# Offsets of the norms and the pool bias added to x by DMAs instead of by GpSimd

## The reference

```python
def reference(x, ...):
    for i in range(DEPTH):
        j = i // N_MIXERS
        if i % N_MIXERS == 0:
            mix = ssd_mixer(x, ...)
        else:
            mix = pool_mixer(x, pool_w[j], pool_b[j], pool_scale[j])
        x = layer_norm(DEEPNORM_ALPHA * x + mix, ln_mix_g[i], ln_mix_b[i])
        x = layer_norm(DEEPNORM_ALPHA * x + sq_relu_mlp(x, mlp_w1[i], mlp_w2[i]), ln_ffn_g[i], ln_ffn_b[i])
    return x
```

## Time and profile before

| | us |
|---|---|
| median of 3 runs | 2206.31 |
| lowest and highest | 2205.95, 2207.38 |
| profiled execution, its own time | 2205.52 |
| profiled execution, span | 2203.8 |

### The profile page before, as it was taken

The page is one execution under the profiler, slowest core; times in us unless marked ns, Lnnn a source line. Parts: engine busy times, 40 slices in busy tenths (PEclk is TensorE's granted clock), DMA queues, the critical chain, the costliest instruction groups (busy, mean ns, idle before and its releaser), DMA issues.

```text
span 2203.8 us, 31261 instructions
## 1 busy us (share of the span) xinstructions
PE 2163.3 (98%) x10626; PEld 1817.0 (82%) x10626; DVE 1439.6 (65%) x1778; ACT 1109.6 (50%) x1549; POOL 234.0 (11%) x172
## 2 busy tenths in 40 slices
PE   9999999999999999999999999989999999999997
PEld 7788888888887778888888888867888888888886
DVE  6787867858768855555565655696565655555656
ACT  5677747757665544444353443446343443443433
POOL 0213322303310500000000000033000000000001
PEclk9999999999999999999999999999999999999999
DMA  8969896988956665555555555446555555555553
GB/s 272 252 202 237 237 278 180 238 230 227 239 183 221 203 212 184 182 200 176 205 190 190 195 185 180 168 152 227 191 191 190 200 181 187 194 180 200 190 191 115
DMA packets 246963, 443.96 MB, mean 201 GB/s; under 512 B 14048, under 2 KB 49040, under 8 KB 245216
## 3 DMA queue, kind: packets, MB, share of 16 engines
q1 hardware_dynamic: 206608, 397.52, 53.8%
q0 software_dynamic: 35664, 28.66, 7.6%
q10 hardware_dynamic: 4608, 16.78, 2.0%
HBM read 440.68 MB, written 2.23 MB: 201 GB/s over the span
## 4 chain that ended last, share of the span: by engine, by line
PE 85%; DVE 7%; DMA 3%; ACT 2%; issue 2%; DVEq 0%; ACTq 0%; SPq 0%
PE acc L357 13%; PE acc L359 13%; PE acc L358 13%; PE acc L608 9%; PE acc L615 5%; PE tb L608 5%; PE sbk L608 5%; DVE wlo L1101 3%; PE sbk L359 3%; PE sbk L357 3%; PE tb L357 3%; PE tb L359 3%; PE tb L358 3%; PE sbk L358 3%; PE sbk L615 2%; PE tb L615 2%
## 5 line engine op out<-in xcount | busy, mean ns | idle before, releaser
L718 ACT CAST whi<-raw 128x1024 fp32r<-128x1024 f32 x746 | 774.8, 1054 | 672.2 <-DMA raw<-in_w 269.8
L1101 DVE TENSOR_TENSOR wlo<-raw,whi 128x1024 fp32r<-128x1024 f32 x746 | 920.4, 1271 | 195.9 <-ACT whi L718 191.4
L357 PE MATMUL acc<-whi,xT 128*128 128x512 f32 x800 | 322.0, 402 | 12.7 <-DVE wlo L1101 10.9
L359 PE MATMUL acc<-wlo,xT 128*128 128x512 f32 x800 | 312.8, 391 | 0.0
L358 PE MATMUL acc<-whi,xT 128*128 128x512 f32 x800 | 312.2, 390 | 0.0
L357 PE MATMUL acc<-whi,hTl 128*128 128x512 f32 x768 | 304.6, 397 | 6.0 <-DVE hTl L1121 3.3
L358 PE MATMUL acc<-whi,hTh 128*128 128x512 f32 x768 | 299.8, 390 | 0.0
L359 PE MATMUL acc<-wlo,hTh 128*128 128x512 f32 x768 | 299.8, 390 | 0.0
L608 PE MATMUL acc<-xT,whi 128*128 128x512 f32 x896 | 224.0, 392 | 0.0
L357 PEld LDWEIGHTS acc<-whi,xT 128*128 128x128 f32 x800 | 150.7, 188 | 49.0 <-issue 9.0
L608 PEld LDWEIGHTS acc<-xT,whi 128*128 128x128 f32 x896 | 162.0, 189 | 29.6
(11 more groups left out here) (207 smaller groups left out, 2675.0 us busy)
## 6 DMA issues: line engine op xcount, KB each, us to landing
raw<-in_w SPq DMA_DIRECT2D x512, 512.0 KB, 4.7
raw<-in_in_proj SPq DMA_DIRECT2D x162, 512.0 KB, 5.4
raw<-in_out_proj SPq DMA_DIRECT2D x64, 512.0 KB, 7.4
spare<-in_masks ACTq DMA_DIRECT2D x16, 512.0 KB, 7.4
spare<-f_scratch POOLq DMA_DIRECT2D x32, 256.0 KB, 15.4
area_d<-in_masks ACTq DMA_DIRECT2D x8, 512.0 KB, 5.9
area_d<-f_scratch POOLq DMA_DIRECT2D x16, 256.0 KB, 6.9
area_c<-in_masks ACTq DMA_DIRECT2D x8, 512.0 KB, 7.2
```

The lines of the kernel that those rows point to most:

```text
L357: pe.matmul(dst, lhs[1][:, kt, rows(t)], hi, start=first and i == 0, stop=False)
L359: mm = pe.matmul(dst, lhs[0][:, kt, rows(t)], lo, start=False, stop=end)
L718: act.copy(whi[:, s.slot(RING)], raw[:, r]).then_inc(hi_ready, 1)
L1101: dve.tensor_tensor(wlo[:, slot], raw[:, r], whi[:, slot].bitcast(F32), ALU.subtract).then_inc(lo_ready, 1)
```

## The change

The sixteen adds at L1681 become four DMAs that add while they write: for each token tile one that reads the row of offsets from HBM, repeated over all partitions, and adds it to x[:, t, :] (1.05 MB each). They signal two new semaphores `offset_in`, and DVE waits for these instead of `x_norm`; `load_gb` no longer waits for the adds. The eight adds at L1704 become four adding DMAs from `psc` to both tiles of x (0.52 MB each), with one semaphore per group. All are issued by GpSimd. The other GpSimd work is the same, and no other engine's instructions are moved. The table `NORMED` of counts goes.

```diff
+        offset_in = [sem(f"offset_in{t}") for t in range(TT)]
...
+        pool_bias = [sem(f"pool_bias{g}") for g in range(4)]
...
-                        sp.wait_ge(x_norm[t], NORMED[t][3] + i + 1)
+                        sp.wait_ge(x_norm[t], i + 1)
...
                 for t in range(TT):
-                    dve.wait_ge(x_norm[t], NORMED[t][i + 1])
+                    dve.wait_ge(offset_in[t], 16 * (i // 2 + 1))
...
-                dve.wait_ge(pool_bias, 2 * g + t + 1)
+                dve.wait_ge(pool_bias[g], 16)
...
                 gain_q3(i)
                 pool.wait_ge(tr_lo, first + 8)
                 for t in range(TT):
-                    for j in range(4):
-                        cs = slice(j * NB, (j + 1) * NB)
-                        pool.tensor_tensor(x[:, t, cs], x[:, t, cs], gb[:, 1, cs], ALU.add).then_inc(x_norm[t], 1)
-                for t in range(TT):
-                    pool.wait_ge(x_norm[t], NORMED[t][i + 1])
+                    pool.dma_start(x[:, t, :], a["ln_b"][i].partition_broadcast(P), accum_op=ALU.add).then_inc(
+                        offset_in[t], 16)
                 load_gb(i + 1)
...
             for g in range(4):
                 pool.wait_ge(tr_done, 8 + 2 * g + 2)
-                for t in range(TT):
-                    cs = slice(g * NB, (g + 1) * NB)
-                    pool.tensor_tensor(x[:, t, cs], x[:, t, cs], psc[:, 1, cs], ALU.add).then_inc(pool_bias, 1)
+                cs = slice(g * NB, (g + 1) * NB)
+                pool.dma_start(x[:, :, cs], psc[:, 1, cs].unsqueeze(1).to_broadcast([P, TT, NB]),
+                               accum_op=ALU.add).then_inc(pool_bias[g], 16)
```

More of the change, by code:

```diff
@@ L102 @@
 TURN_BACK = 2
-NORMED = [[0, 4, 4, 8, 12], [0, 4, 4, 8, 11]]
 LN_BASE = [[0, 10, 20, 30], [0, 11, 21, 32]]
@@ L227, in build @@
         gy_tr, gy_hi, gy_lo, z_silu = sem("gy_tr"), sem("gy_hi"), sem("gy_lo"), sem("z_silu")
-        bands_in, psc_in, bias_scaled, pool_added, pool_bias = (
-            sem(n) for n in ("bands_in", "psc_in", "bias_scaled", "pool_added", "pool_bias"))
+        bands_in, psc_in, bias_scaled, pool_added = (
+            sem(n) for n in ("bands_in", "psc_in", "bias_scaled", "pool_added"))
+        pool_bias = [sem(f"pool_bias{g}") for g in range(4)]
         pool_alpha = sem("pool_alpha")
```

## The result

| | us |
|---|---|
| after, median of 6 runs | 2213.84 (2210.81 to 2218.42) |
| before, median of 6 runs beside them | 2205.66 (2203.70 to 2207.38) |
| ratio | 1.004, 95% interval 1.003 to 1.005 |
| profiled execution after, its time and span | 2217.57, 2215.9 |

The changed kernel is 0.4% slower. The forecast was 2212.5 with a range of 2203 to 2223.

The account below looks back on a forecast made before the run. TensorE, busy 98% of the span, was taken as the bound. A +3, B -0.8 and C +4 give +6.2 us: 2211.7 for the profiled execution, 2212.5 for the median, range 2203 to 2223.

Parts of the forecast that it names:

- C: After the third norm, 1499 to 1540 us: late weight tiles delay the last hidden `hTl` to 1543.5; +4 us.
- A: After the first norm, 736 to 778 us: `hTl` comes at 781 against 778.2; +3 us.
- B: Pool layer, 1438 to 1475 us: 1.9 us gained, 0.3 to 2.2 lost waiting for the last bias DMA; -0.8 us.
- GpSimd's adds block DVE: After both norms: DVE's eight subtractions beside each stretch of GpSimd adds lose about 1 us apiece; at C without cost.
- The price of an adding DMA: At the norms: 87 engine-us per MB, between 46 and 131; two adds take 11.4 us of all 16 engines.
- rival 1: Whole kernel: adds cost like copies, DMA has room; -5.2 to -6.9 us, about 2200; chance 0.2.
- rival 2: Whole kernel: adds cost like 512 B rows; +21 us, 2227; chance 0.18 including what lies toward it.
- The share of the weights beside the adds: After the norms: three weight tiles pass with 2.10 MB of adds, one tile per 5.6 us.
- the timetable: At C: adds end 1517, gains and offsets 1528, fourth weight tile lands about 1521, last `hTl` at 1543.5.
- The upper end of +2.5: Pool layer: +2.5 us if the first bias DMA, behind the `gb` load, also keeps DVE from group 3's tiles.
- The waits without a price: After the norms: DVE's wait on `offset_in` has over 20 us of cover; GpSimd's 0.6 us issues delay nobody.

Follow-up runs that it names:

- plain_copies: Changed kernel with its eight adding DMAs turned into plain copies that overwrite x: 2201.79 us against 2205.15 for the kernel before, ratio 0.9984.
- norms_spread: Kernel before with norm offsets by adding DMAs, gains/offsets loads delayed, psc steps in twelve pieces in later chunks; pool bias on GpSimd: 2200.19 us against 2204.93.
- before_spread: Kernel before with gains/offsets loads delayed and psc steps in twelve pieces in later chunks; all adds on GpSimd: 2200.63 us against 2204.93, ratio 0.9981.
- norm2_only: Kernel before with only norm 2's offsets added by DMAs: 2208.18 us, +2.1 us, ratio 1.0008.
- after_late: Changed kernel with the next gains/offsets loads and undivided psc steps delayed into the second MLP chunk: 2214.62 us, +9.5 us over the kernel before, ratio 1.0042.
- norm0_only: Kernel before with only norm 0's offsets added by DMAs: 2206.47 us, +0.4 us, ratio 0.9998.
- bias_only: Kernel before with only the pool bias by adding DMAs, norm offsets staying on GpSimd: 2208.9 us against 2206.05, ratio 1.0011.
- bias_gb_behind: Kernel before with only the pool bias by adding DMAs, the next gains/offsets load issued behind them: 2207.71 us against 2204.93, ratio 1.0014.
- after_spread: Changed kernel with gains/offsets loads delayed and psc steps in twelve pieces in later chunks: 2205.28 us against 2204.93 for the kernel before, ratio 1.0004.
- norms_only: Changed kernel with the pool bias put back on GpSimd, so only norm offsets use adding DMAs: 2209.91 us, +3.9 us over the kernel before, ratio 1.0016.

## Why the prediction was right, and where it was not

**The sum.** +6.2 was forecast and 8.2 measured, the right sign and the right size. The mechanism at C, weights starved beside dear adds until TensorE's stock is out, was right. That the sum came so near is in part luck: A was forecast 3 us or so too high and B 4 to 6 us too low.

**GpSimd's adds block DVE, and the gain from ending that is small.** Right. Subtractions at 1.16 us appear at 1507. The gain was 3.4 us in `plain_copies` and nothing in `norms_spread` against `before_spread`, where no psc steps follow in stage A.

**The price of an adding DMA.** 87 engine-us per MB was taken between 46 and 131, and 78 measured. This term carried the forecast and held; it rules out rival 1 (copy price) and rival 2 (price of the 512 B rows). The choice of 87 was the middle of two far bounds and not derived, so part of this is luck too. What rival 1 said would happen at the copy price did happen in `plain_copies`, at a smaller size: no stage loses, and the total is 3.4 us faster, where it had said 5.2 to 6.9. B gave 0.3 of its 1.9 us.

**The share of the weights beside the adds.** Wrong. I let three tiles pass per 2.10 MB, as beside the plain loads, one per 5.6 us. Less than one passed in 13.5 us. At first none passed at all, for 5.5 us after the first issue; then the turns went by row, and one added row of 8 KB, 0.63 us, takes the time of six or seven weight rows of 2 KB, 0.09 to 0.10 each. Why the first row came so late was not tested. Since the queue was also through earlier and the four tiles then came within 7 us of each other, the end of the stage was nearly that of the timetable.

**C: +4 forecast, 4.4 in the trace, 2.1 by `norm2_only` (interval -0.2 to 4.0).** Size right, place wrong: the wait is at the first tile of the stock's end (1530.9, `wlo`), not at the last `hTl`. The make-up was wrong as well: the forecast had 4 us of waiting and no clock, and 2.3 us of waiting and 1.7 of clock were measured. Without a dip, in `norm2_only`, C lost 3.0. The forecast took the adds and loads as one sum of engine time, which `after_late` and the spread kernels bear out: it is the two together that exceed the stock. Landings of up to 14.1 us (`after_late`) cost nothing, those of 15.7 to 18.9 cost a wait of 2.3 us.

**A: +3 forecast, +0.4 by `norm0_only` (interval -2.4 to 1.5).** The step that failed is the bottleneck at the end of the stage. The timetable put `hTl` at 781 with its stall. The two waits at the end of the kernel before are gone in the trace after, and two earlier ones stand in their place. Before:

```profile
773.14 0.50 PE L357 MATMUL acc<-whi,hTl 128*128 128x512 f32 x1 [1.18 <-DVE hTl L1121]
778.30 0.53 PE L357 MATMUL acc<-whi,hTl 128*128 128x512 f32 x1 [2.12 <-DVE hTl L1121]
```

and after:

```profile
751.27 0.50 PE L358 MATMUL acc<-whi,xT 128*128 128x512 f32 x1 [2.31 <-DVE wlo L1102]
764.21 0.50 PE L358 MATMUL acc<-whi,xT 128*128 128x512 f32 x1 [2.13 <-DVE wlo L1102]
```

The clock dip is not at 780 any more. Also, A before is not one number: in four profiled executions with GpSimd's adds at that place and the psc steps behind them (the kernel before, `bias_only`, `norm2_only`, `bias_gb_behind`) it took 131.1 to 134.8, in four with adding DMAs 133.9 to 135.3. So a loss of 1 or 2 us at A can't be told from none.

**B: -0.8 forecast, +4.7 in the trace, by the medians +2.9 (`bias_only`) and +5.1 (`after_spread` against `norms_spread`).** The step that failed is the sum of the new waits in this stage. I priced only DVE's wait for the last bias DMA, at 0.3 to 2.2 us, and missed who else uses the DMA engines then. DVE waited once for a bias DMA, 0.7 us, although the last one took 10.0 us to land and not 7.2 to 9.1: it was late itself by then. Two pool weight tiles are issued at the very time at which `gb` and the first bias DMAs are, and everything in the stage hangs on them through DVE's order. The upper end of +2.5 named "keeps DVE from group 3's tiles" but by way of the bias, not of the weights. The clock was left out too: at half for 6.8 us here in the changed kernel and in `bias_only`.

**The waits without a price.** DVE never waited for `offset_in`, as said; the adds landed by 752 and 1522, and DVE reached the waits at 783 and 1552.

## What to carry to other kernels

An adding DMA is not free arithmetic: here it occupied the DMA engines twice as long as a copy, and its cost must be held against the loads that pass at the same time and how long the consumer's stock lasts. Before moving work from an engine into a queue, list what else stands in that queue, and what other queues must bring, within the next 15 us. At C the adds alone, and the loads alone, were free, and both together were not; in the pool layer the adds cost 3 us in either order. And work for which there is no hurry (here the psc steps and the next gains) is best put in small pieces into a stage with slack: that gave 0.2%, and the norms' adding DMAs gave nothing on top of it.

## What the runs showed of the hardware that I had not expected

While a queue of adding rows of 8 KB was served, the other queue's rows of 2 KB got none for 5.5 us after their issue, and then one turn per added row: 215 of them in all beside 256 adds and 86 copied rows, 0.44 MB beside 2.80. With added rows of 2 KB the weights passed at one tile of 0.52 MB per 4 to 5 us. A GpSimd instruction on SBUF held up a DVE one with two SBUF inputs for nearly its whole length, also where the DVE one was short: an `hTl` step of 0.68 us took 5.15. And whether a short wait of TensorE is followed by a dip of the clock differed from place to place and from execution to execution. At C a wait of 2.3 us was followed by 3.4 us at 1.2 GHz in the changed kernel and in `norms_only`, and one of 2.2 us in `norm2_only` was not; at A the changed kernel waited 2.3 and 2.1 us without a dip; in the pool layer the same wait of 1.9 us was followed by a dip in `norms_only` and not in the kernel before.
